# Stick-breaking queries and keys as runs of 512 and 256 columns in two banks, with the second halves copied by ScalarE, added by VectorE and scaled on GpSimd

## The reference

```
qkv = (h @ w_qkv).reshape(B, S, 3, SB_HEADS, SB_HEAD_DIM)
z = einsum('bqhd,bkhd->bhqk', q[:, lo:hi], k[:, :hi]) * scale
log_fail = where(strict, -softplus(z), 0.0)
excl = cumsum(log_fail, axis=3, reverse=True) - log_fail
a = where(strict, exp(log_sigmoid(z) + excl), 0.0)
out = einsum('bhqk,bkhd->bqhd', a, v)
```

## Time and profile before

| | |
|---|---|
| median of 3 runs | 948.44 us (948.07 to 949.13) |
| the profiled execution | 948.44 us, of which the span is 946.7 us |
| PE busy | 934.6 us, 99% of the span |
| DVE busy | 638.3 us, 67% |
| ACT busy | 543.5 us, 57% |
| POOL busy | 57.6 us, 6% |
| granted TensorE clock | 0.999 of full speed |
| DMA | 159.88 MB, mean 169 GB/s |

### The profile page before, as it was taken

One profiled execution on the slowest core, in us unless ns is written; L12 is line 12 of the kernel. 1 busy time (PEld: TensorE's weight loads), 2 busy tenths in 40 slices (PEclk: granted clock), 3 DMA queues, 4 the chain that ended last, 5 costly groups with the idle time before them and its releaser, 6 DMA issues.

```text
span 946.7 us, 14355 instructions
## 1 busy us (share of the span) xinstructions
PE 934.6 (99%) x5412; PEld 812.9 (86%) x5412; DVE 638.3 (67%) x1258; ACT 543.5 (57%) x1044; POOL 57.6 (6%) x110
## 2 busy tenths in 40 slices
PE   9999999999999999999999999999999999999997
PEld 7878788888888998989888888899988898888886
DVE  5888784777776777668666566477964777556664
ACT  6586674658675675557454444466654665444442
POOL 3001330002020020000000000000000000000000
PEclk9999999999999999999999999999999999999999
DMA  9875534554444364435556557664445355655641
GB/s 291 259 193 119 177 134 150 180 178 160 134 123 102 93 217 167 137 133 179 179 192 204 182 180 248 177 190 140 146 167 178 91 180 194 203 179 182 203 171 45
DMA packets 109584, 159.88 MB, mean 169 GB/s; under 512 B 10734, under 2 KB 45900, under 8 KB 109260
## 3 DMA queue, kind: packets, MB, share of 16 engines
q1 hardware_dynamic: 109080, 158.40, 53.6%
q10 hardware_dynamic: 436, 0.56, 0.2%
HBM read 156.32 MB, written 2.11 MB: 167 GB/s over the span
## 4 chain that ended last, share of the span: by engine, by line
PE 95%; DVE 3%; ACT 1%; issue 1%; DMA 0%; SPq 0%; DVEq 0%; ACTq 0%
PE bank L498 23%; PE bank L500 23%; PE bank L499 23%; PE bank L1204 9%; PE bank L1207 5%; PE bank L640 3%; PE bank L654 2%; PE bank L552 2%; PE bank L666 2%; PE bank L679 1%; PE bank L625 1%; DVE w_lo L1967 1%; PE bank L1345 1%; PE bank L680 0%; DVE xT L2025 0%
## 5 line engine op out<-in xcount | busy, mean ns | idle before, releaser
L1967 DVE TENSOR_TENSOR w_lo<-raw,w_hi 128x1024 fp32r<-128x1024 f32 (+3 forms) x296 | 335.1, 1176 | 136.2 <-ACT w_hi L1423 135.8
L1423 ACT CAST w_hi<-raw 128x1024 fp32r<-128x1024 f32 (+3 forms) x296 | 281.7, 1011 | 128.5 <-DMA raw<-in_mlp_w_in 71.9
L498 PE MATMUL bank<-w_hi,xT 128*128 128x512 f32 (+1 forms) x366 | 145.3, 397 | 1.3 <-issue 0.8
L500 PE MATMUL bank<-w_hi,xT 128*128 128x512 f32 (+1 forms) x366 | 141.3, 386 | 0.0
L499 PE MATMUL bank<-w_lo,xT 128*128 128x512 f32 (+1 forms) x366 | 140.8, 385 | 0.0
L498 PE MATMUL bank<-w_hi,hT_hi 128*128 128x512 f32 (+1 forms) x348 | 136.4, 392 | 0.3
L500 PE MATMUL bank<-w_hi,hT_lo 128*128 128x512 f32 (+1 forms) x348 | 134.9, 388 | 0.0
L499 PE MATMUL bank<-w_lo,hT_hi 128*128 128x512 f32 (+1 forms) x348 | 134.9, 388 | 0.0
L498 PE MATMUL bank<-xT,w_hi 128*128 128x256 f32 x368 | 106.0, 288 | 0.3 <-DVE w_lo L1967 0.3
L1204 PE MATMUL bank<-xT,w_hi 128*128 128x512 f32 x384 | 104.5, 394 | 0.0
L500 PE MATMUL bank<-xT,w_lo 128*128 128x256 f32 x368 | 104.1, 283 | 0.0
(11 more groups left out here) (273 smaller groups left out, 1302.9 us busy)
## 6 DMA issues: line engine op xcount, KB each, us to landing
raw<-in_mlp_w_in SPq DMA_DIRECT2D x32, 1024.0 KB, 5.2
raw<-in_mlp_w_out SPq DMA_DIRECT2D x32, 1024.0 KB, 5.1
raw<-in_w_in_ab SPq DMA_DIRECT2D x13, 1024.0 KB, 11.2
raw<-in_w_in_cd SPq DMA_DIRECT2D x13, 1024.0 KB, 5.1
raw<-in_xa_w_kv SPq DMA_DIRECT2D x8, 1024.0 KB, 5.2
raw<-in_sb_w_qkv SPq DMA_DIRECT2D x16, 512.0 KB, 4.7
raw<-in_w_out_ab SPq DMA_DIRECT2D x4, 1024.0 KB, 5.2
raw<-in_w_out_cd SPq DMA_DIRECT2D x4, 1024.0 KB, 5.2
```

The source lines that it names most:

```text
L498: pe.matmul(o, wh, ih, start=start, stop=False, skip_group_check=True)
L500: return pe.matmul(o, wl, ih, start=False, stop=stop, skip_group_check=True)
L1423: nc.scalar.copy(w_hi[:, u % SLOTS, a], raw[:, u % SLOTS, a]).then_inc(hi_ready, 1)
L1967: V.tensor_tensor(w_lo[:, u % SLOTS, a], raw[:, u % SLOTS, a], w_hi[:, u % SLOTS, a].bitcast(F32), ALU.subtract).then_inc(lo_ready, 1)
```

## The change

PE makes queries and keys of a head in two banks, `2 * (h % 2) + n`, in place of one of four. In each bank w_hi runs against 512 columns (xT hi and lo of a chunk together), 8 times, and w_lo against 256 columns, 8 times, into the first half. The result is the sum of the two halves of the bank. ACT copies the second half into `sb_qk(h)` (`sqk_second`, 256 columns, twice for a head), DVE adds the first half to it in place (256 columns, twice), and GpSimd multiplies the 512 columns in place by `row`, once for each head. `sqk_ready` now comes from GpSimd. The banks are free again with DVE's addition (`sqk_summed`).

```diff
@@ PE
-                b = h % 4
-                begin(("sqk", h), b)
+                wh, wl = (flat(w, u).rearrange("p (c n) -> p c n", n=S) for w in (w_hi, w_lo))
                 for n in range(2):
-                    ins = features("", banks[b][:, n * S:(n + 1) * S], u, KC, 256, n * P, X, r, True)
+                    b = 2 * (h % 2) + n
+                    begin(("sqk", h, n), b)
+                    a = slice(n * P, (n + 1) * P)
+                    for c in range(KC):
+                        pe.wait_ge(*r(c))
+                        pe.matmul(banks[b][:, :], wh[:, c, a], xT[:, c].rearrange("p a s -> p (a s)"), start=c == 0, stop=False, skip_group_check=True)
+                    for c in range(KC):
+                        ins = pe.matmul(banks[b][:, 0:S], wl[:, c, a], xT_hi[:, c, :], start=False, stop=c == KC - 1, skip_group_check=True)
+                    if n == 0:
+                        end(("sqk", h, 0), ins, (sqk_summed, 2 * h + 1))
                 ins.then_inc(units_used, 1)
-                end_with_unit(("sqk", h), u, (sqk_ready, h + 1))
+                end_with_unit(("sqk", h, 1), u, (sqk_summed, 2 * h + 2))
@@ ACT
+            def sqk_second(h):
+
+                for n in range(2):
+                    ps = condition(act, ("sqk", h, n))
+                    own.sig(nc.scalar.copy(sb_qk(h)[:, n * S:(n + 1) * S], ps[:, S:2 * S]), sqk_copied)
+
             used(U["sqk", 0])
+            sqk_second(0)
             used(U["sqk", 1])
+            sqk_second(1)
...
                     own.sig(nc.scalar.activation(sbuf_of(1, i), sbuf_of(1, i), ACT.Ln, bias=1.0), sb_log)
+                if i + 2 < HEADS:
+                    sqk_second(i + 2)
@@ DVE
                 used(U["sqk", h])
-                ps = condition(dve, ("sqk", h))
-                own.sig(V.tensor_tensor(two_halves(sb_qk(h)), two_halves(ps[:, :]), row2, ALU.mult), sqk_ready)
+                for n in range(2):
+                    dve.wait_ge(sqk_copied, 2 * h + n + 1)
+                    o = sb_qk(h)[:, n * S:(n + 1) * S]
+                    own.sig(V.tensor_tensor(o, condition(dve, ("sqk", h, n))[:, 0:S], o, ALU.add), sqk_summed)
@@ GpSimd, behind its work for the first layer
+            pool.wait_ge(row_ready, row_no["x", 1])
+            for h in range(HEADS):
+                pool.wait_ge(sqk_summed, 2 * h + 2)
+                own.sig(G.tensor_tensor(two_halves(sb_qk(h)), two_halves(sb_qk(h)), row2, ALU.mult), sqk_ready)
```

More of the change, by code:

```diff
@@ L274, in build @@
         sqk_ready, hiT_ready, loT_ready = sem("sqk_ready"), sem("hiT_ready"), sem("loT_ready")
+        sqk_copied, sqk_summed = sem("sqk_copied"), sem("sqk_summed")
         scratch_ready = sem("scratch_ready")
```

## The result

The changed kernel takes 953.88 us (median of 5 runs, 953.34 to 954.81), against 948.44 for the kernel before in the same comparison. The ratio is 1.0057, with a 95% interval of 1.0046 to 1.0068: 5.4 us slower. The profiled execution took 954.54 us, its span is 952.7. I had forecast +2.5 us and a range up to 953.0, so the direction was right and the size was not.

A forecast was written before the change was run, and what follows sets the result against it. PE's own work was taken as the bound (busy 934.6 of 946.7 us). A stall of 3.95 us from GpSimd's contention and the longer chain, less 1.44 saved, gave +2.5 on 948.44: 950.9 us, range 946.9 to 953.0.

The forecast's parts named there:

- PE's saving: Query and key products on PE: wide products shorten each head by 0.18 us, 1.44 us for eight heads.
- The longer chain through ScalarE: VectorE's loop per head: ScalarE's copies and the additions start the next chain at 4.95 us against 4.40, 0.55 more.
- What GpSimd does to VectorE: Shared SBUF: GpSimd's multiplication slows VectorE by 0.65 us a head over the chain, 0.84 in iterations with `memT_lo`.
- The 0.56: VectorE's loss per us of overlap with GpSimd, read at 335 us as 0.80 us lost in 1.42.
- p: VectorE's loss in one head from GpSimd's work: 0.65 or 0.84 us, with bounds 0 and 1.5.
- my own formula: PE's total stall by head 5 is 6p - 0.33 us, forecast 3.95; less 1.44 saved gives +2.5.
- "PE's stall" at the turning of the weights: PE turning weights of heads 4 and 5 waits for ACT's exponential: 5p - 0.08, then 6p - 0.33 us in all.
- The clock: A lower granted PE clock after stalls would add time that no row of before shows; no size given.
- (d): Rival: VectorE stands for GpSimd's whole time, p over 0.95; +6 us, 954.5 us; chance 0.1.
- The row at 335.69: VectorE difference under a busy GpSimd, 1.02 us against 0.49; taken as showing that VectorE did move on.
- (a): Rival: no contention for VectorE's chain, p = 0, head 4's wait just met, only PE's saving left; 947.0 us; chance 0.15.
- (b): Rival: half the loss on VectorE, p of 0.2 to 0.45, stalls 0.9 to 2.4 us; 948 to 949.4 us; chance 0.2.

The follow-up runs named there:

- the run with the spare tile: Changed kernel with GpSimd's multiplications made in a tile nobody reads, the scaling left out, and scores waiting for VectorE's second addition; 954.68 us, ratio 1.0066.
- the second try with early memT pieces: Changed kernel, complete, with the first four memT pieces moved from iteration 3 to iteration 0, on VectorE behind the weight unit; 952.79 us, ratio 1.0040.
- the first try: Changed kernel, complete, with the first four memT pieces moved from iteration 3 to iteration 0, on VectorE ahead of the weight unit; 954.23 us, ratio 1.0060.

## Why the prediction was right in direction and wrong in size

**PE's saving, 0.18 us a head and 1.44 in all: right.** PE goes from scores to scores in 660.24 - 653.03 = 7.21 us where it took 7.39, and the products alone bring 1.5 us (0.17 a head by their trace). The other estimate, 0.04 us a head by the figures of the Trainium skill (TensorE: Matmul & The Clock Gate, section Back-to-back issue gap), would have given 0.3 us: this case's runs don't agree with it.

**The longer chain through ScalarE, 0.55 us a head: right.** DVE's loop without POOL is 7.13 us (655.66 - 648.53 from sums to sums in the run without multiplications), worked out as 7.14.

**What GpSimd does to VectorE: that it holds VectorE up is right, how much is wrong.** I took 0.65 for the heads where POOL lies over the running sums, because they go at half the rate, and 0.84 for those with `memT_lo`. Measured are 0.97 and 1.04. The step that failed is "so they ask for the memory less", with the 0.56 us of loss for each us of overlap behind it. Both take it that DVE goes on at a lower rate. The rows of single operations show something else. These are the two sums of head 1 in the changed kernel:

```profile
649.83 1.40 DVE L2634 TENSOR_TENSOR_SCAN arena<-arena 128x128 f32<-128x128 f32 x1
651.15 0.66 DVE L2634 TENSOR_TENSOR_SCAN arena<-arena 128x256 f32<-128x256 f32 x1
```

Without GpSimd's operation they take 0.42 and 0.67. So the whole loss, 0.98 us, falls on the one sum that starts while POOL (649.41 to 650.94) is at work, and the other loses nothing. It is the same over `memT_lo`: of four pieces the second goes from 0.48 to 1.52 us, and the others keep 0.47 to 0.49. One DVE operation stands still for about a microsecond, and a share of DVE's rate doesn't come into it. That is why the slower sums lose as much as the faster pieces.

The 0.56 was also misread: POOL was at work again from 335.50 us, so the overlap with the operation of 335.02 to 335.78 was 0.68 us and not 0.40, and the two rows give 0.80 in 1.70, or 0.47.

With p at 0.97 and 1.04, 6p is 5.96 in place of 4.28, and my own formula gives a stall of 5.6 us and +4.2 us, so this term was short by 1.7 us. That alone, 952.6 us, would still lie in my range.

**"PE's stall" at the turning of the weights: the wrong wait.** I read the distance between ACT's exponential and PE's turning, 2.7 us, and took it for the tightest. It wasn't. Two rows of the kernel before, which I hadn't laid side by side, from the timelines of DVE and PE:

```profile
674.85 0.41 DVE L2023 TENSOR_TENSOR hT_lo<-bank,hT_hi 128x256 fp32r<-128x256 f32 x1
```

```profile
676.86 0.59 PE L679 MATMUL bank<-pt,arena 128*128 128x256 f32 x2
```

Bank 7 is freed at 675.26 and wanted again at 676.86, a slack of 1.6 us. It hangs on the same chain, as `y_lo` stands in DVE's order behind `sb_w` and the scores. Worked out with it (`sb_w` must then end by 674.3 for head 4, 1.17 us before what I had asked) the run without POOL should stall 675.4 - 674.3 = 1.1 us, where my own sum had no stall at all. It did stall, at line 680, by 0.9 us, which was also what I expected ahead of that run. So in the changed kernel the stall is by this wait, 3 x 0.97 + 2 x 1.04 + 0.9 = 5.9 us by head 3's values. The three waits, each taken as the time from the scores to line 680 less the 0.66 us that it takes without a wait, are 0.76 + 2.53 + 2.56 = 5.85 us. One more stands behind them at full clock, for head 4's values: 0.62 us by the same measure in the run with the spare tile.

**The sum again.** At full clock, as in the run with the spare tile, PE waits four times, 0.74 + 2.56 + 2.55 + 0.62 = 6.47 us. Each start after a wait costs it some 0.08 us more (6.65 us from line 680 to the next scores against 6.56 with the products alone), 0.3 in all. Less 1.44 of saving this is +5.3, and the medians lie 5.4 apart. In the profiled execution of the changed kernel it is 5.85 of waiting, 0.2 for the starts and 1.5 for the lower clock (8.23 us from line 680 to the next scores, against 6.74 before), less 1.44: +6.1, for 6.0 of longer span. Of the 2.9 us that my +2.5 was short, p accounts for 1.7 and the wrong wait for most of the rest.

**The clock.** I had named it as something that no row could size, and gave it nothing. Its net price is less than the 1.5 us, as PE would have spent part of them in the fourth wait. Four traces give it. From line 680 for head 3's values to line 680 for head 4's, PE takes 690.27 - 681.38 = 8.89 us in the changed kernel and 688.87 - 679.99 = 8.88 in the second try with early memT pieces, both with the lower clock. It takes 689.86 - 681.77 = 8.09 in the run with the spare tile and 689.45 - 681.35 = 8.10 in the first try, both without. That is 0.8 us where it falls. Whole executions scatter by more than this. The mean granted clock of one suggests whether it had such a stretch: in the spare tile's run those at 0.999 took 954.22 and 954.48 us, those at 0.997 955.72 and 954.88. Of the changed kernel's five, four are at 0.997 (953.34 to 954.81) and one is at 0.999, with 953.88 right among them, so its median of +5.4 doesn't tell +5.3 from +6.1. Why the clock falls in some executions and not in others stays open.

**The rivals.** (d), with p over 0.95, is the one that came, and I gave it 0.1. Its mechanism, that DVE stands, is also what the single rows show, though for 0.97 to 1.04 us and not for POOL's whole 1.5. The row at 335.69 didn't speak against it: 1.02 us for an operation of 0.49 is what a stop looks like too. Its time of 954.5 was for p of 1.3. With the right wait p of 0.97 is enough. (a) and (b) fall with the running sums at 1.98 us. "The wait of head 4 is just met" in (a) was wrong as well: without POOL the kernel comes to 947.8, not 947.0.

## What to carry to other kernels

Work moved to GpSimd isn't free because GpSimd is idle. Ask what VectorE does at that moment: if it works on two SBUF tiles and is on the way to what PE waits for, 512 columns with two inputs cost it a full microsecond, more than doing them itself (0.7). The same operation costs VectorE nothing beside operations of its that read PSUM, so a wait that puts it there can be worth more than the operation's place in the queue.

When a chain grows, list all that PE takes from it, the release of a bank too, and not only the result that the chain is for. Slack is the smallest of these distances. Gains of 0.18 us a head are lost to any one of them.

## What the runs showed of the hardware

- Where a two-input multiplication of 512 columns on GpSimd lay beside VectorE operations with two inputs in SBUF, one VectorE operation was held up whole and the rest kept their time: a running sum of 128 columns went from 0.42 to 1.40 us, or the second of four scalar-tensor-tensor operations from 0.48 to 1.52. GpSimd's own time grew from 1.30 to 1.53 us.
- A one-input operation of 512 columns on GpSimd lasts longer, 1.66 us, and takes only 0.28 to 0.36 us from VectorE.
- The VectorE operation that had begun before GpSimd's was never slowed: 0.55 us for the first of the chain, though POOL's operation began, by the trace, 0.16 us after it. Together with GpSimd's own longer time this looks as if each lets an operation of the other end first; that is read from the rows, and not tested.
- PE's granted clock fell to half after two waits of 2.4 us, 7.5 us of work between them, and was back 3.0 us after PE resumed. After the same two waits in the run with the spare tile (2.40 and 2.39 us) it did not fall; in the run with the multiplication on VectorE it fell after one of 1.98.
